# Twenty-four gate columns computed as rows of tokens beside the value columns, an earlier distance bias, and another order at both ends of a two-block transformer kernel

## The chip, the cores and the metric

The kernel runs on one core of a Trainium2 chip. The metric is the time of one launch on the device in microseconds (us). The engines are named as in the profile: PE (matrix engine; PEld is its weight load), DVE (vector), ACT (scalar), POOL (GpSimd), SP (issues most transfers). DVEq, ACTq, SPq are the queues on which an engine issues transfers.

## What is computed

Two transformer blocks over T = 512 tokens of width D = 1024, all in float32. The first block projects the normed rows and mixes two attentions, the second has a short convolution, a sparse attention with a distance bias and a feed-forward network. Of the first block, what matters here is:

```python
h = rms_norm(x, norm_g)
dq, dk, dv, dz, nq, nkv, nz, ng = jnp.split(h @ w_in, IN_SPLITS, axis=-1)   # dv: 512 columns, ng: 24
o_diff = diff_attention(rms_norm(dq), rms_norm(dk), dv, lam, slopes)
o_cmp, p_cmp = compressed_attention(nq, kc, vc)     # softmax over 31 compressed keys
...
g = jax.nn.sigmoid(ng)                              # three gates for each of 8 heads
o_nsa = g[0] * o_cmp + g[1] * o_slc + g[2] * o_win
x = x + concatenate([o_diff * silu(dz), o_nsa * silu(nz)]) @ w_out
```

Of the second block it is `bias = rel_bias[rel_bucket(distance)]`, a table of 32 x 8 looked up at 640 distances, made in the kernel as a product with a one-hot matrix, and at the very end `rms_norm_2(x, g_final)`, written out by rows.

## The kernel before

**Products.** Every projection is split so that float32 is kept: an operand is its rounded part (hi) plus the rest (lo), and a product of a 128-row k-tile is three matmuls, hi with hi, lo with hi, hi with lo (L1847). Weights come in units of up to 2048 columns per partition (1 MB). For each unit SP loads `raw` (two slots, used in turn), ACT rounds it to `w_hi` (L1084), POOL subtracts to get `w_lo` in pieces of 512 columns (L1024), and PE multiplies. For units that run beside an attention DVE makes the low pieces (L1703) instead. Two layouts exist. In a feature unit the weights are stationary and the 512 tokens move, so a tile is (up to 128 features) x 512. In a token unit (`token=True`) 128 tokens are stationary and the columns of the weights move; its four tiles are (128 tokens) x (columns).

**Order of work.** A plan is built in Python and each engine walks it. `order` (L208) lists the units, `project` emits the matmuls of a unit in steps of `size` k-tiles, and each step calls `tick`. What follows a unit is put in with `later(n, ...)`, n steps on. Each engine executes its entries strictly in plan order, waiting on semaphores.

**Units around the change.** After the NSA queries (`nq_u`) come the gate unit `ng_u` (the 24 gate columns with 96 neighbours, 120 columns as features, which makes tiles of 120 x 512), the NSA keys `nk_u` (kind `kd`), the two units of differential values `dv_u` (token units of 4 k-tiles x 512 columns), then the NSA values `nv_u` beside the differential attention.

- Gates: ACT takes the tanh of the tile (L1114), PE turns it by four transposes (L1874), DVE scales the turned 128 x 96 block into `ngt` (L1465).
- Norms of queries and keys (`NORM`): ACT squares (L1116, L1117, L1119), PE sums over the 64 rows of a head (L1888), ACT takes the root (L1146, L1147; the square root needs a table load where another function came between), DVE inverts (L1452, 128 x 512), POOL multiplies (L1034). For `kd`, DVE multiplies too (L1457, two of 64 x 512).
- Compressed scores: `scores(b)` for b = 0, 1. Part 0 is 16 matmuls on PE (32 records, L2056), part 1 masks and subtracts the maximum on DVE (L1599 to L1605), part 2 is the exponential on ACT (L1301), part 3 on DVE sums, inverts, multiplies with the gate and scales (L1609, L1610, L1612, L1614, L1615).
- The differential attention's first scores (L1906) follow the last value unit.

**Start.** PE runs 18 idle products as warm-up (L2064, 36 records), with the transpose of the first norm's gains after the 13th (L2067). DVE copies these gains (L1364), squares token row tile 1 (L1678) and scales the four row tiles (L1641); PE transposes them (L1798). Small arrays come by SP in a row of transfers (L958). The distance bias is made in the first projection: two products of `relb` with `onehot` (L2122, four records), copied by ACT (L1311).

**Tail of the NSA attention.** `split_high` and `split_low("mix", m)` make the hi and lo parts of the mixed rows for the output projection; the low part is DVE's L1737, which runs in plan order among the copies of turned probabilities (L1543) for which PE's products (L1978) wait.

**End.** The last product fills the final 256 columns in a tile of tokens. DVE and ACT scale the last row tile by halves of 512 columns (L1658, L1153), and SP issues two transfers, L1008 and then L1010.

## Time and profile before

| what | us |
|---|---|
| median of 3 runs | 1067.86 (1067.71 to 1067.88) |
| the profiled execution, its own time | 1068.18 |
| its span | 1066.4 |
| PE busy (5457 matmul records) | 1055.5 (99%) |
| PEld busy | 835.8 (78%) |
| DVE busy | 499.6 (47%) |
| ACT busy | 458.9 (43%) |
| POOL busy | 400.5 (38%) |
| chain that ended last: PE / DVE / ACT | 91% / 5% / 2% |

The profiled execution took 1.8 us more than its span, and 0.3 us more than the median of the runs. The busy time of a matmul record is modelled and overlaps its neighbour's; what a matmul costs in a stream is the distance from its start to the next one's start. The granted clock of PE was 1.00 in all 40 slices.

### The profile page before, as it was taken

What the parts mean: (1) busy time and instruction counts of PE and PEld (TensorE: products, weight loads), DVE (VectorE), ACT (ScalarE), POOL (GpSimd) and SP (SyncE); (2) the same over time, 40 slices, a digit from 0 to 9 for tenths busy, and PEclk for the clock granted to TensorE, in tenths of its full rate; (3) what the DMA queues carried; (4) which work ended last, traced back from release to release, by engine and by line L of the source; (5) the groups of instructions that cost most, each with busy time, mean ns of one, the idle gap of its engine ahead of it and who ended that gap; (6) DMA issues with size and microseconds to landing.
All of it is one profiled execution on the core that took longest, in us unless ns stands there. A gap on an engine that the chain in (4) does not pass through costs nothing.

```text
span 1066.4 us, 14261 instructions
## 1 busy us (share of the span) xinstructions
PE 1055.5 (99%) x5457; PEld 835.8 (78%) x5457; DVE 499.6 (47%) x1047; ACT 458.9 (43%) x789; POOL 400.5 (38%) x300
## 2 busy tenths in 40 slices
PE   9999999999999999999999999999999999999997
PEld 7777776867678876888777888888888888888886
DVE  5754798675671515998588235240000000032444
ACT  6455657676663524323366423342222122233533
POOL 3554630001023352545100154533534444465772
PEclk9999999999999999999999999999999999999999
DMA  9532221111123232232221223223232332322221
...
DMA packets 83667, 96.09 MB, mean 90 GB/s; under 512 B 8089, under 2 KB 68722, under 8 KB 83610
## 3 DMA queue, kind: packets, MB, share of 16 engines
...
## 4 chain that ended last, share of the span: by engine, by line
PE 91%; DVE 5%; ACT 2%; issue 1%; POOL 0%; DVEq 0%; ACTq 0%; POOLq 0%
PE bank L1847 54%; PE bank L2160 22%; PE bank L1906 4%; PE bank L1937 3%; PE bank L1978 3%; DVE L L1452 1%; PE bank L1954 1%; PE bank L1798 1%; PE bank L2135 1%; PE bank L2011 1%; DVE L L1502 1%; PE bank L2064 1%; PE bank L1888 0%; DVE w_lo L1703 0%; DVE pool L1457 0%
## 5 line engine op out<-in xcount | busy, mean ns | idle before, releaser
L1024 POOL TENSOR_TENSOR w_lo<-raw,w_hi 128x512 fp32r<-128x512 f32 (+1 forms) x190 | 268.4, 1442 | 440.6 <-ACT w_hi L1084 428.2
L1847 PE MATMUL bank<-h_hi,w_hi 128*128 128x512 f32 (+1 forms) x584 | 234.6, 402 | 0.5 <-POOL w_lo L1024 0.4
L1847 PE MATMUL bank<-h_hi,w_lo 128*128 128x512 f32 (+1 forms) x584 | 228.1, 391 | 0.0
L1847 PE MATMUL bank<-h_lo,w_hi 128*128 128x512 f32 (+1 forms) x584 | 227.2, 390 | 0.0
L1084 ACT ACTIVATE w_hi<-raw 128x512 fp32r<-128x512 f32 (+3 forms) x94 | 112.0, 1221 | 119.2 <-PE bank L1847 116.8
L1062 POOL TENSOR_TENSOR w_lo<-raw,w_hi 128x512 fp32r<-128x512 f32 x88 | 110.7, 1290 | 133.5 <-ACT w_hi L1329 67.1
L2160 PE MATMUL bank<-h_hi,w_hi 128*128 128x512 f32 x352 | 137.1, 389 | 0.0
L2160 PE MATMUL bank<-h_hi,w_lo 128*128 128x512 f32 x352 | 137.0, 389 | 0.0
L2160 PE MATMUL bank<-h_lo,w_hi 128*128 128x512 f32 x352 | 136.8, 389 | 0.0
L1847 PEld LDWEIGHTS bank<-h_hi,w_hi 128*128 128x128 f32 (+1 forms) x584 | 109.2, 187 | 34.0 <-issue 9.6
L1847 PE MATMUL bank<-w_hi,h_hi 128*128 128x512 f32 x333 | 129.8, 390 | 0.0
L1847 PE MATMUL bank<-w_hi,h_lo 128*128 128x512 f32 x333 | 129.6, 389 | 0.0
L1847 PE MATMUL bank<-w_lo,h_hi 128*128 128x512 f32 x333 | 129.6, 389 | 0.0
L1847 PEld LDWEIGHTS bank<-h_hi,w_lo 128*128 128x128 f32 (+1 forms) x584 | 109.2, 187 | 24.1
L1847 PEld LDWEIGHTS bank<-h_lo,w_hi 128*128 128x128 f32 (+1 forms) x584 | 109.4, 187 | 21.7 <-DVE h_lo L1745 0.4
L1783 DVE TENSOR_TENSOR pool<-bank,L 128x512 f32 (+1 forms) x22 | 15.2, 692 | 215.7 <-PE bank L2160 215.7
L2160 PEld LDWEIGHTS bank<-h_hi,w_hi 128*128 128x128 f32 x352 | 66.1, 188 | 14.0 <-ACT h_hi L1285 0.2
L2160 PEld LDWEIGHTS bank<-h_hi,w_lo 128*128 128x128 f32 x352 | 66.1, 188 | 13.7
L2160 PEld LDWEIGHTS bank<-h_lo,w_hi 128*128 128x128 f32 x352 | 66.1, 188 | 13.6
L1232 ACT ACTIVATE L<-L,st 128x128 f32<-128x128 f32 (+3 forms) x128 | 70.3, 555 | 13.5 <-DVE st L1502 13.5
L1847 PEld LDWEIGHTS bank<-w_hi,h_hi 128*128 128x128 f32 x333 | 62.5, 188 | 13.8 <-issue 1.0
L1847 PEld LDWEIGHTS bank<-w_lo,h_hi 128*128 128x128 f32 x333 | 62.5, 188 | 13.0
...
## 6 DMA issues: line engine op xcount, KB each, us to landing
...
```

The costliest lines, as they stand in the source:

```text
L1024: nc.gpsimd.tensor_tensor(w_lo[:, u.n % 2, cols], raw[:, u.n % 2, cols], w_hi[:, u.n % 2, cols].bitcast(F32), ALU.subtract).then_inc(lo_do ...
L1062: nc.gpsimd.tensor_tensor(w_lo[:, n % 2, cols], raw[:, n % 2, cols], w_hi[:, n % 2, cols].bitcast(F32), ALU.subtract).then_inc(lo_done, 1)
L1084: act_fn(w_hi[:, u.n % 2, cols], raw[:, u.n % 2, cols], ACT.Copy).then_inc(hi_done, 1)
L1232: ins = act_fn(x, x, ACT.Exp, scale=-1.0, bias=stat(ST_MN, job, c, p), accum_out=stat(ST_SM, job, c, p))
L1452: v.reciprocal(r, r).then_inc(recip_done, 1)
L1502: ins = v.tensor_tensor_reduce(out=x, in0=src, in1=bias, scale=factor, scalar=3e38, op0=ALU.add, op1=ALU.min, accum_out=stat(ST_MN, job, c ...
L1783: v.tensor_tensor(x, bank[2 + j][:, :], L[:, j, :], ALU.mult).then_inc(act_done, 1)
L1847: ins = mm(bank[t.bank][0:t.m, :], stationary, moving, start=first and n == 0, stop=last and n == len(products) - 1, skip_group_check=u.token)
L1906: ins = mm(bank[S_BANKS[c]][:, columns(job, p)], q, k, start=True, stop=True)
L1937: ins = nc.tensor.transpose(dst[:, o:o + P], L[:, (job.r + c) % LRING, o:o + P], ident)
L1978: ins = mm(O[DH * half:DH * half + DH, P * i:P * i + P], x, turned(job.t + half)[:, o:o + P], start=dsa and j == 0, stop=j == i and (dsa o ...
L2160: ins = mm(bank[2 * j + m][:, :], w[:, k, P * m:P * m + P], x[:, k, :], start=n == 0, stop=n == len(products) - 1)
```

## The change

1. The gate unit is gone. The 512 value columns come in three token units in place of two: 8 k-tiles x 256 columns, then twice 4 k-tiles x 280 columns (256 of the values and the 24 of the gates, loaded by a second transfer). ACT evacuates 256 columns of each tile and takes the tanh of the 24 straight into `ngt`; DVE scales `ngt` once (`gates`).
2. Part 3 of the compressed scores moves: b = 0 behind the differential attention, b = 1 ten steps later, inside the NSA attention. `scores(0)` and `scores(1)` come two steps later each.
3. The bias products move behind 14 idle products (18 before), the transpose after the 10th; `relb` and `onehot` are loaded by ACT's queue instead of SP's; DVE makes the two copies between token row tiles 0 and 1.
4. In the tail of the NSA attention the four `split_low` go from steps 4, 5, 6, 7 (each behind the step) to behind 5, behind 6, before 7 and behind 7, in the order m = 0, 1, 2, 3.
5. At the end the halves are 384 columns for ACT and 640 for DVE, and ACT issues the transfer of its own part.

```diff
-    ng_u = Unit("nsa_gate", [(rows_of(w1in, 0, ND, C_NG - 96, 120), 0, 120)], ND, 120, [Tile(0, 120, "ng", 0)])
-    dv_u = token_units("diff_v", w1in, C_DV, "dv", 0)
+    dv_u = [Unit("diff_v", [(rows_of(w1in, 0, ND, C_DV, 256), 0, 256)], ND, 256,
+                 [Tile(0, P, "dv", (0, i)) for i in range(NT)], token=True)]
+    gate_tiles = [Tile(0, P, "dv_ng", (1, i)) for i in range(NT)]
+    dv_u += [Unit("diff_v_nsa_gate", [(rows_of(w1in, k, 4, C_DV + 256, 256), 0, 256), (rows_of(w1in, k, 4, C_NG, 24), 256, 24)],
+                  4, 280, gate_tiles, k0=k, first=k == 0, last=k == 4, token=True) for k in (0, 4)]
...
-    order = (dq_u[:1] + [kv_u] + dk_u[:1] + dq_u[1:] + dk_u[1:] + nq_u + [ng_u, nk_u] + dv_u + [nv_u] + nz_u + z_u
+    order = (dq_u[:1] + [kv_u] + dk_u[:1] + dq_u[1:] + dk_u[1:] + nq_u + [nk_u] + dv_u + [nv_u] + nz_u + z_u
...
-    NORM, AUX_COPY = ("dq", "dk", "nq", "kd"), ("vd", "ng", "viw")
+    NORM, AUX_COPY = ("dq", "dk", "nq", "kd"), ("vd", "viw")
...
-            return
-        if group[0].kind == "ng":
-            later(2, lambda: [aux(t) for t in group])
-            later(4, lambda: [finish(t) for t in group])
...
+    left[0], left[4] = [("rows_done", 1)], [("rows_done", 2)]
...
-        bias_tiles = []
         col_waits, left[COL_BANK] = left[COL_BANK], [("col_done", 2)]
-        for j in range(2):
-            t = Tile(0, DSA_HEADS, "rows", j)
-            t.bank, t.waits = 6 + j, left[6 + j]
-            t.done = upto("tile_done")
-            left[t.bank] = [("rows_done", j + 1)]
-            bias_tiles.append(t)
-        emit("small_arrays", tiles=bias_tiles, waits=col_waits)
+        emit("small_arrays", waits=col_waits)
...
         emit("cmp", b=b, part=0, waits=waits)
-        for part in range(1, 4):
+        for part in range(1, 3):
             later(part, lambda part=part: emit("cmp", b=b, part=part, waits=None))
     later(2, cmp_values)
-    project(nq_u + [ng_u], RING4, 4)
-    later(1, lambda: scores(0))
-    later(5, lambda: scores(1))
-    project([nk_u] + dv_u, RING4, 4)
+    project(nq_u, RING4, 4)
+    later(3, lambda: scores(0))
+    later(7, lambda: scores(1))
+    project([nk_u], RING4, 4)
+    project(dv_u, RING4, 8)
...
     attend("diff", steps_left["diff"])
+    emit("gates")
+    emit("cmp", b=0, part=3, waits=None)
+    later(10, lambda: emit("cmp", b=1, part=3, waits=None))
...
             split_high("mix", at - 1)
+        if at == 7:
+            split_low("mix", 2)
         attend("nsa")
-        if 4 <= at < 8:
-            split_low("mix", at - 4)
+        if 5 <= at < 8:
+            split_low("mix", (0, 1, 3)[at - 5])
...
-        LAST_BANK = 4
+        LAST_BANK, LAST_COLS = 4, 384
...
+        table_in, rows_mm = sem("table_in"), sem("rows_mm")
...
-            sp.dma_start(out[0, T - P:T, 512:D], zs[:, NT - 1, 512:D]).then_inc(out_done, 16)
-            sp.wait_ge(y_act, NT)
-            sp.dma_start(out[0, T - P:T, 0:512], zs[:, NT - 1, 0:512]).then_inc(out_done, 16)
+            sp.dma_start(out[0, T - P:T, LAST_COLS:D], zs[:, NT - 1, LAST_COLS:D]).then_inc(out_done, 16)
...
-                    act_fn(dv[:, idx[1], :], src, ACT.Copy).then_inc(sc_evac, 1)
+                    act_fn(dv[:, idx[1], 0:256], src[:, 0:256], ACT.Copy).then_inc(sc_evac, 1)
+                if kind == "dv_ng":
+                    act_fn(dv[:, idx[1], 256:T], src[:, 0:256], ACT.Copy)
+                    act_fn(ngt[:, idx[1], :], src[:, 256:280], ACT.Tanh, scale=0.5).then_inc(sc_evac, 1)
...
             def scaled(i):
-                x = zs[:, i, 0:D if i < NT - 2 else 512]
+                x = zs[:, i, 0:D if i < NT - 2 else LAST_COLS]
                 sc.wait_ge(recip_last, i + 1)
                 act_fn(x, x, ACT.Copy, scale=st[:, ST_RR + i:ST_RR + i + 1]).then_inc(y_act, 1)
+                if i == NT - 1:
+                    sc.wait_ge(y_act, NT)
+                    sc.dma_start(out[0, T - P:T, 0:LAST_COLS], x).then_inc(out_done, 16)
...
             sc.dma_start(vec_rows[R_NORM:R_NORM + ND, :], a["norm_g"][0].rearrange("(r c) -> r c", c=P)).then_inc(first_in, 16)
+            sc.dma_start(relb[:, :], a["rel_bias_2"]).then_inc(table_in, 16)
+            sc.dma_start(onehot, a["onehot"]).then_inc(table_in, 16)
...
-                    for j, t in enumerate(e["tiles"]):
-                        w = T if j == 0 else BIASW - T
-                        sc.wait_ge(tile_done, t.done)
-
-                        act_fn(bias_row[:, T * j:T * j + w], bank[t.bank][0:DSA_HEADS, 0:w], ACT.Copy, scale=-1.0)\
-                            .then_inc(rows_done, 1)
...
-                elif t.kind == "ng":
-                    v.tensor_scalar(ngt[:, :, :], blocks[:, :, 96:120], 0.25, 0.25, ALU.mult, ALU.add).then_inc(aux_copied, 1)
...
                     ve.wait_ge(recip_last, i + 1)
-                    v.tensor_scalar(zs[:, i, 512:D], zs[:, i, 512:D], r, None, ALU.mult).then_inc(y_done, 1)
+                    x = zs[:, i, LAST_COLS:D]
+                    v.tensor_scalar(x, x, r, None, ALU.mult).then_inc(y_done, 1)
...
                     normed_row(nth, i)
+                    if i == 0:
+                        for j, w in enumerate((T, BIASW - T)):
+                            ve.wait_ge(rows_mm, j + 1)
+                            v.tensor_scalar(bias_row[:, T * j:T * j + w], bank[4 * j][0:DSA_HEADS, 0:w], -1.0, None, ALU.mult)\
+                                .then_inc(rows_done, 1)
...
                                            ALU.mult, ALU.mult).then_inc(kc_done, 1)
+                if kind == "gates":
+                    ve.wait_ge(sc_evac, gate_tiles[-1].sc)
+                    chain(v.tensor_scalar(ngt[:, :, :], ngt[:, :, :], 0.25, 0.25, ALU.mult, ALU.add))
...
-                        pe.wait_ge(sc_evac, dv_u[1].tiles[-1].sc)
+                        pe.wait_ge(sc_evac, gate_tiles[-1].sc)
...
             pe.wait_ge(zero_done, 1)
-            for n in range(18):
+            for n in range(14):
                 mm(bank[4][:, 0:P], idle_rows, idle_rows, start=True, stop=True)
-                if n == 12:
+                if n == 13:
+                    pe.wait_ge(table_in, 32)
+                    for j, w in enumerate((T, BIASW - T)):
+                        mm(bank[4 * j][0:DSA_HEADS, 0:w], relb[:, :], onehot[:, T * j:T * j + w], start=True, stop=True)\
+                            .then_inc(rows_mm, 1)
+                if n == 9:
...
-                    for j, t in enumerate(e["tiles"]):
-                        w = (T, BIASW - T)[j]
-                        wait_free(pe, t.waits)
-                        mm(bank[t.bank][0:DSA_HEADS, 0:w], relb[:, :], onehot[:, T * j:T * j + w], start=True, stop=True)\
-                            .then_inc(tile_done, 1)
```

What the planner does with it stands in the rows of the program's order. First **POOL from the NSA queries to the end of the values**. `pool<-pool,L` is the norm multiplication of two query tiles, `pool<-zs,L` that of the two key tiles, eight or four `w_lo` pieces are one or two units. Before:

```order
L1024 TENSOR_TENSOR w_lo<-raw,w_hi 128x512 [waits hi_done]
L1024 TENSOR_TENSOR w_lo<-raw,w_hi 128x448 [waits hi_done]
L1034 TENSOR_TENSOR pool<-pool,L 128x512 [waits ve_evac,recip_done] x2
L1024 TENSOR_TENSOR w_lo<-raw,w_hi 128x512 [waits hi_done] x8
L1034 TENSOR_TENSOR pool<-pool,L 128x512 [waits ve_evac,recip_done] x2
L1024 TENSOR_TENSOR w_lo<-raw,w_hi 128x512 [waits hi_done] x4
L1034 TENSOR_TENSOR pool<-zs,L 128x512 [waits ve_evac,recip_done] x2
L1024 TENSOR_TENSOR w_lo<-raw,w_hi 128x512 [waits hi_done] x4
```

And with the change:

```order
L1020 TENSOR_TENSOR w_lo<-raw,w_hi 128x512 [waits hi_done] x4
L1030 TENSOR_TENSOR pool<-pool,L 128x512 [waits ve_evac,recip_done] x2
L1020 TENSOR_TENSOR w_lo<-raw,w_hi 128x512 [waits hi_done] x4
L1030 TENSOR_TENSOR pool<-pool,L 128x512 [waits ve_evac,recip_done] x2
L1020 TENSOR_TENSOR w_lo<-raw,w_hi 128x512 [waits hi_done] x2
L1020 TENSOR_TENSOR w_lo<-raw,w_hi 128x96 [waits hi_done]
L1030 TENSOR_TENSOR pool<-zs,L 128x512 [waits ve_evac,recip_done] x2
L1020 TENSOR_TENSOR w_lo<-raw,w_hi 128x512 [waits hi_done] x2
L1020 TENSOR_TENSOR w_lo<-raw,w_hi 128x96 [waits hi_done]
L1020 TENSOR_TENSOR w_lo<-raw,w_hi 128x512 [waits hi_done] x4
```

Before, all weights of the values were split ahead of the key norm's two multiplications. Now those of the third value unit (the second row pair of 512 and 96) stand behind them.

**ACT, with the change, from the first value unit to the third** (L1120 evacuates 256 value columns, L1303 is the exponential of the compressed scores, L1143 and L1144 are the key norm's roots, L1080 the high part of the third value unit):

```order
L1120 ACTIVATE pool<-bank 128x256 [waits tile_done]
L1303 ACT_TABLE_LOAD
L1303 ACTIVATE pool<-pool 128x16x31 [waits cmp_lg_done]
L1120 ACTIVATE pool<-bank 128x256 [waits tile_done]
L1143 ACT_TABLE_LOAD
L1143 ACTIVATE L<-bank,st 64x512 [waits aux_done]
L1144 ACTIVATE L<-bank,st 64x512
L1143 ACTIVATE L<-bank,st 64x512
L1144 ACTIVATE L<-bank,st 64x512
L1120 ACTIVATE pool<-bank 128x256 [waits tile_done] x2
L1080 ACTIVATE w_hi<-raw 128x1120 [waits tile_done,raw_in0]
```

The key roots now stand behind the second token tile of the first value unit; before, they stood behind no evacuation of a value tile.

**DVE inside the NSA attention, with the change** (L1527 scales probabilities, L1603 to L1609 are part 3 for b = 1, L1621 scales the differential output, L1496 takes PE's next scores):

```order
L1527 TENSOR_SCALAR L<-L,st 128x256 [waits dve_step]
L1527 TENSOR_SCALAR L<-L,st 128x256 x3
L1603 TENSOR_REDUCE st<-pool 128x16 [waits cmp_ex_done]
L1604 RECIPROCAL st<-st 128x16 [waits dve_step]
L1606 TENSOR_TENSOR st<-st,ngt 128x16 [waits dve_step]
L1608 TENSOR_TENSOR pool<-pool,const 128x16x31 [waits dve_step]
L1609 TENSOR_TENSOR pool<-pool,st 128x16x31 [waits dve_step]
L1621 TENSOR_TENSOR pool<-pool,st 128x512 [waits diff_recip]
L1703 TENSOR_TENSOR w_lo<-raw,w_hi 128x512 [waits hi_done]
L1496 ISA L,st<-bank,pool 128x512 [waits tr_done,s_done]
```

Before, the rows L1603 to L1609 (there L1609 to L1615) were not in this place; L1627, L1703 and L1502, their counterparts there, followed directly on the four L1533.

## Rows read from the trace of the kernel before

**Rows 1.** PE's waits (us, times, longest us); then the page's loads (busy, mean ns).

```profile
PE bank L1906 <- DVE st L1502: 1.6, 5, 0.5
...
PE bank L1798 <- DVE zs L1641: 0.9, 1, 0.9
PE bank L1978 <- DVE pool L1543: 0.5, 1, 0.5
PE bank L1847 <- POOL w_lo L1024: 0.4, 1, 0.4
...
L1847 PEld LDWEIGHTS bank<-h_hi,w_hi 128*128 128x128 f32 (+1 forms) x584 | 109.2, 187 | 34.0 <-issue 9.6
```

**Rows 2.** Chain in three windows: start us, us, what.

```profile
17.22 1.17 PE bank L2122 x4
...
118.69 1.91 PE bank L2056 x32
...
123.54 0.41 PE bank L1874 x4
...
427.52 95.42 PE bank L1847 x420
```

**Rows 3.** Busy time in 1058.08 to 1060.12 us: length, PE, PEld, DVE, ACT, POOL, clock, DMA.

```profile
1058.08:1060.12 2.04, 2.04 (x19) 2.03 (x17) 1.68 (x4) 1.81 (x4) 0.00 (x0) 1.00 0.63 257
```

**Rows 4.** PE's timeline: start us, us, what, [idle before <-releaser].

```profile
114.86 0.40 PE L1847 MATMUL bank<-h_hi,w_lo 128*120 128x512 f32 x1
115.70 0.47 PE L1847 MATMUL bank<-h_hi,w_hi 128*128 128x512 f32 x1 [0.44 <-POOL w_lo L1024]
...
154.27 1.14 PE L1906 MATMUL bank<-pool 64*128 64x128 f32 x8
...
231.90 1.14 PE L1906 MATMUL bank<-pool 64*128 64x128 f32 x8
```

**Rows 5.** POOL's timeline.

```profile
122.01 5.04 POOL L1024 TENSOR_TENSOR w_lo<-raw,w_hi 128x512 fp32r<-128x512 f32 x4 [2.72 <-ACT w_hi L1084]
...
132.72 5.87 POOL L1024 TENSOR_TENSOR w_lo<-raw,w_hi 128x512 fp32r<-128x512 f32 x4 [2.73 <-ACT w_hi L1084]
142.47 1.79 POOL L1034 TENSOR_TENSOR pool<-zs,L 128x512 f32<-128x512 f32 x1 [3.88 <-DVE L L1452]
```

**Rows 6.** ACT's timeline, a table load and a root.

```profile
115.91 1.28 ACT L1146 ACT_TABLE_LOAD   x1
117.21 0.68 ACT L1146 ACTIVATE L<-bank,st 64x512 f32<-64x512 f32 x1
```

**Rows 7.** DVE's timeline around 140 and 150 us.

```profile
139.04 3.34 DVE L1452 RECIPROCAL L<-L 128x512 f32<-128x512 f32 x1
142.42 2.38 DVE L1457 TENSOR_TENSOR pool<-zs,L 64x512 f32<-64x512 f32 x2
...
150.64 0.67 DVE L1609 TENSOR_REDUCE st<-pool 128x16 f32<-128x496 f32 x1
...
153.15 2.49 DVE L1703 TENSOR_TENSOR w_lo<-raw,w_hi 128x512 fp32r<-128x512 f32 x4
```

**Rows 8.** DVE's timeline in the NSA attention.

```profile
210.23 0.69 DVE L1397 SCALAR_TENSOR_TENSOR zs<-zs,bank 128x512 f32<-128x512 f32 x1 [2.18 <-ACT zs L1124]
...
230.28 0.69 DVE L1502 CUSTOM_DVE_ANT_0 L<-bank,pool 128x512 f32<-128x512 f32 x1 [0.45 <-PE bank L1937]
```

**Rows 9.** DVE's timeline at the start.

```profile
7.16 0.17 DVE L1364 COPY col<-bank 128x8 f32<-128x8 f32 x1 [6.28 <-PE bank L2067]
7.24 1.22 DVE L1678 CUSTOM_DVE_ANT_0 zs<-xres 128x1024 f32<-128x1024 f32 x1
...
11.76 1.01 DVE L1641 TENSOR_SCALAR zs<-xres,st 128x128 f32<-128x128 f32 x3
```

**Rows 10.** The end: ACT's last operation and the last transfer's issue.

```profile
1062.77 0.72 ACT L1153 ACTIVATE zs<-zs,st 128x512 f32<-128x512 f32 x1 [0.23 <-DVE st L1655]
...
1063.67 0.43 SPq L1010 DMA_DIRECT2D out<-zs  x1
```

10 lines of the change are left out of this document (3 added, 7 removed).

## The prediction

> **What bounds it now.** I read first the busy shares (PE 99% of the span), then PE's waits. Behind its warm-up PE stands still on nothing but four pairs of lines [rows 1]: at the start for `zs`, at one weight unit for POOL's `w_lo`, five times for DVE's scores in the attentions, once for the copies of turned probabilities. They make 3.4 us in all. So the time is the sum of what PE streams, and the change is worth what it takes from or adds to that stream, plus the waits that it opens or closes. What other engines save is worth nothing unless PE waits for them. PE's stream has a fixed pace: in a long stretch of 512-column matmuls 420 take 95.42 us [rows 2], so one costs 0.227 us.
>
> **The sum, part by part.**
>
> *The gate unit goes.* It has 8 k-tiles x 3 products = 24 matmuls of 512 tokens; 24 x 0.227 = 5.45 us. Its four transposes are 0.41 [rows 2]. Both lie in PE's stream: **-5.86**. With them go the tanh, DVE's scaling of a bank and 960 columns of `w_lo`, all off the path, at 0, with one exception: the norm multiplication and the next unit's `w_lo` came too late for PE at 115.70. The last gate matmul starts at 114.86, and 0.227 later the next should have [rows 4]: 0.6 us lost. POOL's work comes in another order now (four `w_lo` pieces of the keys, then the queries' two multiplications), so the piece no longer stands behind DVE's inverse: **-0.6**.
>
> *The value units.* Before: 2 units x 4 k-tiles x 4 token tiles x 3 = 96 matmuls of 512 columns, 21.8 us. After: 96 of 256 and 96 of 280. The only narrow matmuls of this kind are in the last unit: between the first start at 1058.08 and the last at 1060.12 lie 17 intervals (the row counts 19 records, a neighbour's among them), 0.120 us each [rows 3]. For 280 I take 0.130 (0.120 x 280/256). 96 x 0.120 + 96 x 0.130 = 24.0: **+2.2**.
>
> *Bias products.* Their four records take 1.17 us of the first projection [rows 2] and move to the time in which PE waits for `zs` (0.9 us, plus four idle products fewer): **-1.2**. The new hazard: they wait for two transfers issued on ACT's queue among the large loads of the rows.
>
> *The start.* DVE idles 6.28 us until PE has turned the gains, and squares row 1 right behind, for 1.22 us [rows 9]. The transpose comes three idle products sooner, so this chain can start about 1 us earlier. But DVE now copies the bias between rows 0 and 1 (two operations; 0.3 to 0.7 us each by the copy of 8 columns, 0.17 [rows 9], and the 512-column one of 0.69 [rows 8]) and may wait there for the bias products, with the scaling of rows 1 to 3 queued behind. Row 3 starts at 11.76 now [rows 9]. Bounds -1.0 (the whole head start) and +1.0 (the table loads as late as the last row tile); I take **-0.4**, since rows 1 to 3 also wait for their own loads.
>
> *A new wait at the third value unit.* Its `w_lo` stands behind the key norm's multiplications on POOL, and these behind ACT's roots, which now stand behind the evacuation of the first value unit's second token tile. From the end of that tile the chain is: evacuation and hand-overs 0.3; table load 1.28 and a pair of roots 2 x 0.69 [rows 6]; inverse 3.34, DVE's multiplications 2.38, second inverse 3.34 [rows 7]; POOL's multiplication 1.79 and one piece of `w_lo` 1.47 as beside a busy DVE, 5.87/4 [rows 5]. That is 15.3 us. PE meanwhile does token tiles 2 and 3 (2 x 24 x 0.120 = 5.8), the second unit (48 x 0.130 = 6.2) and compressed scores (1.91 [rows 2]): 13.9. So it arrives 1.4 us early, and the second piece, needed two k-tiles in, costs about 0.9 more: **+2.3**. Bounds: 0 if ACT gets the roots out earlier, 3.5 if each step slips by a few tenths. The high part of the NSA values, behind the second exponential on ACT, has the third unit's 6.2 us as cover.
>
> The Trainium skill, "SBUF — State Buffer", section "SBUF: two separate sides", says that the port pair of VectorE and GpSimd is an exclusive lock and the loser blocks for a whole instruction. Here POOL's multiplication ran 1.79 us while DVE's two took 2.38, started 0.05 apart [rows 5, 7]: against 5.04/4 = 1.26 for one of POOL's operations of this size undisturbed: slower by 0.5, not blocked. By the rule, `w_lo` would wait for one more whole DVE multiplication, 1.2 us, and this term would be 3.3 or so.
>
> *Part 3 of the compressed scores.* It is taken from DVE ahead of the first differential scores (2.50 us for b = 1, 150.64 to 153.15 [rows 7]), where DVE was close behind PE but never waited for. It is put into the NSA attention. For b = 0 (2.75 with the scaling of the gates) there is a cover: DVE idles 2.18 us before 210.23 [rows 8], and the half microsecond left over falls before PE's next need. For b = 1 DVE's chain runs to the products of 231.90 [rows 4] with only 0.45 idle [rows 8] and about 1.0 us between its last score and PE's need. 2.5 - 0.45 - 1.0 = **+1.1**. Bounds 0 and 2.5.
>
> *Tail of the attention.* PE waits 0.5 us once for DVE's copy L1543 [rows 1], which stands behind two low parts. Moved earlier, they leave it free: **-0.6** with the restart; bounds -0.7 and 0 (the moved ones may block an earlier copy).
>
> *The end.* ACT's last operation, 512 columns, ends at 1063.49; SP issues the last transfer at 1063.67 [rows 10]. With 384 columns it is about 0.1 shorter, and ACT issues at once: **-0.2**. DVE's 640 columns add under 0.1 and end before ACT.
>
> Sum: -5.86 - 0.6 + 2.2 - 1.2 - 0.4 + 2.3 + 1.1 - 0.6 - 0.2 = **-3.3 us**; in the profile 1068.2 becomes 1064.9. That execution was 0.3 above the median of the runs, so against the median: 1067.86 - 3.3 = **1064.6**.
>
> **Rivals.** A difference under 0.2%, 2.1 us, is about what a measurement of this kernel cannot tell from none.
>
> 1. *The waits eat the gain.* Third value unit 3.5, part 3 of b = 1 2.5, no head start: -3.3 + 1.2 + 1.4 + 0.4 = -0.3, **1067.5**, no change. For it: two serial chains were priced without slack. Against: all would have to go wrong together.
> 2. *No new waits.* If ACT and DVE run ahead in both places and the start gains 1.0: -3.3 - 2.3 - 1.1 - 0.6 = -7.3, **1060.6**. For it: PE's waits on DVE are few now [rows 1]. Against: the chain of 15.3 us consists of measured steps.
> 3. *Slower: narrow matmuls are paced by their weight loads.* A token unit of 256 columns needs as many weight loads as one of 512. In the last unit PEld is busy 2.03 of 2.04 us with 17 loads [rows 3], 0.12 a load, so that queue is full there. If PE could not start the next load before the last one's whole 0.187 us [rows 1] were over, 192 x 0.187 = 35.9 in place of 24.0: +11.9, the result +8.6, **1076.5**. It decides from a spacing of 0.153 us: (3.3 + 2.1)/192 = 0.028 above the mean of 0.125. Against it: the same row shows 19 matmuls in 2.04 us, which no pace of 0.187 allows. The Trainium skill, "TensorE: Matmul & The Clock Gate", section "Back-to-back issue gap", says that spacing is set by both operations, the load and the matmul; the row agrees with loads overlapping each other or the matmul here. It is a short stretch, though, and a stream of 192 is not seen.
>
> **Numbers.** The forecast's own case 0.50, with 1063.0 to 1065.7 as its range; no new waits 0.25; waits eat the gain 0.20; narrow matmuls 0.05. Faster: 0.50 + 0.25 = 0.75; within 0.2%: 0.20; slower: 0.05. The range takes in the forecast, most of rivals 1 and 2, and leaves out rival 3 and the ends of the others: 1061.4 to 1067.4.
>
> **What would show it.** Matmul starts 0.120 and 0.130 us apart in the value units, 24 matmuls and 4 transposes fewer. No PE wait on `w_lo` at the key unit, but one of 1 to 2.5 us at the third value unit, with the key norm's multiplications ending just before on POOL. PE's first scores about 3.6 us earlier than 154.27 [rows 4] (5.86 + 0.6 + 1.2 + 0.4 less 2.2 and 2.3). A wait of about 1 us on DVE near 230 behind part 3, and none on L1543 in the tail. The forecast is wrong if the narrow matmuls are over 0.14 apart, or if the bias transfers land late and PE starts its transposes after 9.4.

## The result: 0.24% slower, where 0.3% faster was predicted

| | before | with the change |
|---|---|---|
| median of 12 runs each, us | 1067.88 (1067.71 to 1068.31) | 1070.57 (1069.17 to 1071.36) |
| profiled execution, its own time, us | 1068.18 | 1070.57 |
| its span, us | 1066.4 | 1068.7 |

The ratio is 1.0024 [1.0016, 1.0032]: slower by 2.7 us, where -3.3 was forecast. So 6 us have to be found. The executions also spread over 2.2 us instead of 0.6, and the mean granted clock of PE is 0.994 to 0.997 in them, where the profiled execution of before had 1.00.

**The waits.** With the change, PE's waits and the load that stood in [rows 1] (columns as there):

```profile
PE bank L1909 <- DVE st L1496: 2.8, 6, 1.1
PE bank L1850 <- POOL w_lo L1020: 2.5, 2, 1.9
...
PE bank L2071 <- DMA PT<-in_onehot: 0.8, 1, 0.8
PE bank L1801 <- DVE zs L1635: 0.8, 1, 0.8
PE bank L1909 <- ACT ngt L1123: 0.6, 1, 0.6
PE bank L1850 <- ACT h_hi L1287: 0.2, 1, 0.2
...
L1850 PEld LDWEIGHTS bank<-h_hi,w_hi 128*128 128x128 f32 (+1 forms) x576 | 107.7, 187 | 32.9 <-issue 10.3
```

The wait for DVE's copy in the tail is gone; the one for `w_lo` went from 0.4 to 2.5 and now lies at the third value unit; four are new: `onehot`, `ngt`, a short one of 0.2 for `h_hi` ahead of the first projection, and a sixth of 1.1 on L1909. Together they are 7.7 us against 3.4, so 4.3 more, in a stream that is shorter by 3.8 (5.86 us of gate matmuls and transposes less, 2.1 more in the values). That makes +0.5; the other 1.8 us of the 2.3 between the spans lie where no wait is listed.

**The start.** The chain that ended last, 0 to 16 us (start us, us, what):

```profile
2.16 6.25 DMA PT<-in_onehot
...
8.46 1.03 PE bank L2071 x2
...
9.52 0.88 DVE L L1680 x2
...
10.50 0.76 DVE zs L1635
...
11.31 3.30 PE bank L1801 x16
```

and DVE's timeline (start, length, what, [idle before]), which answers to [rows 9]:

```profile
5.88 0.17 DVE L1360 COPY col<-bank 128x8 f32<-128x8 f32 x1 [5.00 <-PE bank L2075]
...
9.52 0.88 DVE L1680 TENSOR_SCALAR L<-bank 8x512 f32<-8x512 f32 x2 [1.43 <-PE bank L2071]
...
10.50 0.75 DVE L1635 TENSOR_SCALAR zs<-xres,st 128x1024 f32<-128x1024 f32 x1
```

The gains are copied 1.28 us sooner (5.88 against 7.16). But the bias products stood for `onehot`, which had taken 6.25 us to land; DVE's copies stood for the products, and the scaling of row 1 (10.50) behind the copies. DVE wins its head start at the gains and loses all of it, and more, at 9.52.

How large the head start is depends on the warm-up, and this pair shows it at its largest. PE's timeline of the kernel before, and that of a later version with the same start (the tail undone, below):

```profile
1.00 5.91 PE L2064 MATMUL bank<-vc 128*128 128x128 f32 x26 [1.00 <-POOL vc L1036]
```

```profile
1.00 4.68 PE L2073 MATMUL bank<-vc 128*128 128x128 f32 x26 [1.00 <-POOL vc L1039]
```

The same 26 records took 5.91 us before, and 4.68 to 5.01 in the four profiled executions of later versions with the old start (start undone, all four repaired, end undone, tail undone). Those copied the gains at 5.88 to 6.21 instead of 7.16, so against them the 5.88 above is 0.0 to 0.3 sooner. They also passed the place of the first projection where before is at 18.32 at 17.87 to 18.06. So the profiled execution of before is 0.3 to 0.5 us behind them at the start, and what is read against it makes the change look better by as much.

**The clock.** Busy time in six stretches (columns as in [rows 3]; the number behind POOL's is the granted clock):

```profile
10.00:12.00 2.00, 1.20 (x8) 0.96 (x7) 1.93 (x6) 1.87 (x5) 0.00 (x0) 0.66 1.10 364
12.00:14.00 2.00, 2.00 (x11) 2.00 (x11) 1.19 (x5) 0.03 (x1) 0.62 (x1) 0.50 0.64 182
...
146.00:148.00 2.00, 1.00 (x4) 0.77 (x5) 1.93 (x3) 0.00 (x0) 2.00 (x3) 0.80 0.00 0
148.00:150.00 2.00, 2.00 (x10) 2.00 (x10) 0.80 (x3) 1.66 (x3) 0.39 (x1) 0.50 0.25 36
150.00:152.00 2.00, 2.00 (x15) 2.00 (x15) 1.45 (x4) 1.52 (x5) 0.00 (x0) 0.85 1.01 332
...
1060.29:1062.33 2.04, 2.04 (x19) 2.03 (x17) 1.68 (x4) 1.81 (x4) 0.00 (x0) 1.00 0.63 257
```

Twice PE falls to the lower of its two levels (0.50, 1.2 GHz) at a pair of standstills: the two of 0.8 us at the start, and those of the third value unit. In finer windows the fall comes at about 10.7 and 147.2, each time just after the second standstill has begun. Before, both stretches were at 1.00. No wait is recorded for it: PE is "busy" 2.00 of 2.00 us and does half the work. The last row answers to [rows 3] and is the same as there, record for record.

**The value units.** PE's timeline:

```profile
123.75 0.28 PE L1850 MATMUL bank<-w_hi,h_hi 128*128 128x256 f32 x1
...
126.15 0.28 PE L1850 MATMUL bank<-w_lo,h_hi 128*128 128x256 f32 x1
...
139.00 0.29 PE L1850 MATMUL bank<-w_hi,h_hi 128*128 128x280 f32 x1
...
142.08 0.29 PE L1850 MATMUL bank<-w_hi,h_hi 128*128 128x280 f32 x1
...
144.26 0.29 PE L1850 MATMUL bank<-w_lo,h_hi 128*128 128x280 f32 x1
146.42 0.40 PE L1850 MATMUL bank<-w_hi,h_hi 128*128 128x280 f32 x1 [1.87 <-POOL w_lo L1020]
...
147.66 0.60 PE L1850 MATMUL bank<-w_hi,h_hi 128*128 128x280 f32 x1 [0.58 <-POOL w_lo L1020]
148.06 0.43 PE L1850 MATMUL bank<-w_hi,h_lo 128*128 128x280 f32 x1
148.29 0.43 PE L1850 MATMUL bank<-w_lo,h_hi 128*128 128x280 f32 x1
...
155.59 1.14 PE L1909 MATMUL bank<-pool 64*128 64x128 f32 x8 [0.56 <-ACT ngt L1123]
...
234.43 1.14 PE L1909 MATMUL bank<-pool 64*128 64x128 f32 x8 [1.12 <-DVE st L1496]
```

From 123.75 to 126.15 are 20 intervals, 0.120 each; from 139.00 to 142.08 are 24, 0.128 each. At 148 one takes 0.23. The last two rows answer to [rows 4]. The first value matmul starts at 123.40, where it started at 129.27 before.

What PE waited for at 146.42 stands in POOL's timeline, and what POOL waited for in DVE's (beside [rows 5, 7]):

```profile
137.10 1.79 POOL L1030 TENSOR_TENSOR pool<-zs,L 128x512 f32<-128x512 f32 x1 [7.75 <-DVE L L1448]
142.90 1.78 POOL L1030 TENSOR_TENSOR pool<-zs,L 128x512 f32<-128x512 f32 x1 [4.01 <-DVE L L1448]
144.64 3.74 POOL L1020 TENSOR_TENSOR w_lo<-raw,w_hi 128x512 fp32r<-128x512 f32 x3
```

```profile
133.66 3.35 DVE L1448 RECIPROCAL L<-L 128x512 f32<-128x512 f32 x1 [5.82 <-ACT L L1144]
...
139.47 3.35 DVE L1448 RECIPROCAL L<-L 128x512 f32<-128x512 f32 x1
```

The first inverse starts behind ACT's roots (L1144), which a table load at 130.96 precedes; then the second inverse, POOL's multiplication and `w_lo` follow: the chain of the prediction, link by link.

**The end.** ACT's last operation and its transfer, beside [rows 10]:

```profile
1065.05 0.62 ACT L1150 ACTIVATE zs<-zs,st 128x384 f32<-128x384 f32 x1 [0.23 <-DVE st L1649]
1065.69 0.37 ACTq L1153 DMA_DIRECT2D out<-zs  x1
```

**Where the difference stands.** The same events of PE in both traces, as start with the change less start before: +0.86 in the first projection (19.18, 18.32), +0.83 at 99.80, +1.32 at the first scores (155.59, 154.27), +1.33 at 210.39, +2.53 at the scores of 234.43 (231.90), +2.07 in the output projection (313.51, 311.44), +2.21 at the last matmul (1062.33, 1060.12), +2.3 in the span. The start, the values, part 3 and the tail each have their step in this list. Against the four other executions of the old start the step of the start is 1.1 to 1.3 rather than 0.86.

### The profile page after: what moved, and what is told of

It reads as the page before. It is cut to its first block, busy times and chain, and to the rows that moved or that the text cites. A ratio compares the mean times of both kernels' runs of the same rounds, so it can differ in the third digit from the quotient of the medians.

```text
span 1068.7 us, 14387 instructions
## 1 busy us (share of the span) xinstructions
PE 1053.5 (99%) x5517; PEld 839.2 (79%) x5517; DVE 497.5 (47%) x1049; ACT 455.2 (43%) x792; POOL 399.3 (37%) x300
## 4 chain that ended last, share of the span: by engine, by line
PE 93%; DVE 3%; ACT 2%; issue 1%; DMA 1%; POOL 0%; ACTq 0%; DVEq 0%
PE bank L1850 56%; PE bank L2163 22%; PE bank L1909 4%; PE bank L1940 3%; PE bank L1981 3%; PE bank L1957 1%; PE bank L2138 1%; PE bank L1801 1%; DVE L L1496 1%; PE bank L2014 1%; PE bank L1891 1%; DVE L L1448 1%; DMA PT<-in_onehot 1%; PE bank L1970 0%; PE bank L1933 0%
## 5 line engine op out<-in xcount | busy, mean ns | idle before, releaser
L1850 PE MATMUL bank<-h_hi,w_hi 128*128 128x512 f32 (+1 forms) x576 | 231.3, 402 | 0.3 <-ACT h_hi L1287 0.2
L1850 PE MATMUL bank<-h_hi,w_lo 128*128 128x512 f32 (+1 forms) x576 | 225.0, 391 | 0.0
L1850 PE MATMUL bank<-h_lo,w_hi 128*128 128x512 f32 (+1 forms) x576 | 224.0, 390 | 0.0
L1080 ACT ACTIVATE w_hi<-raw 128x512 fp32r<-128x512 f32 (+3 forms) x94 | 111.4, 1214 | 114.0 <-PE bank L1850 113.2
L1850 PE MATMUL bank<-w_hi,h_hi 128*128 128x512 f32 (+2 forms) x365 | 136.7, 374 | 2.5 <-POOL w_lo L1020 2.5
L1850 PE MATMUL bank<-w_hi,h_lo 128*128 128x512 f32 (+2 forms) x365 | 136.1, 373 | 0.0
L1850 PE MATMUL bank<-w_lo,h_hi 128*128 128x512 f32 (+2 forms) x365 | 136.0, 373 | 0.0
L1850 PEld LDWEIGHTS bank<-w_hi,h_hi 128*128 128x128 f32 x365 | 69.3, 190 | 15.6 <-POOL w_lo L1020 2.9
L1850 PEld LDWEIGHTS bank<-w_hi,h_lo 128*128 128x128 f32 x365 | 69.2, 190 | 11.8
L1850 PEld LDWEIGHTS bank<-w_lo,h_hi 128*128 128x128 f32 x365 | 69.2, 190 | 11.8
```

The lines of the kernel that those rows point to most:

```text
L1080: act_fn(w_hi[:, u.n % 2, cols], raw[:, u.n % 2, cols], ACT.Copy).then_inc(hi_done, 1)
L1850: ins = mm(bank[t.bank][0:t.m, 0:u.width if u.token else T], stationary, moving, start=first and n == 0, stop=last and n == len(products) ...
```

## The experiments

Diffs are against the changed kernel, unless said otherwise. The kernel before ran beside each, with medians of 1067.8 to 1068.0. A difference "against the change" is against 1070.57.

**The start undone.** `relb` and `onehot` back on SP's queue, the bias products in the first projection, the copies by ACT, 18 idle products.

```diff
-            for n in range(14):
+            for n in range(18):
...
-                if n == 9:
+                if n == 12:
...
-            sc.dma_start(relb[:, :], a["rel_bias_2"]).then_inc(table_in, 16)
-            sc.dma_start(onehot, a["onehot"]).then_inc(table_in, 16)
...
+                small(relb[:, :], a["rel_bias_2"])
+                small(onehot[:, :], a["onehot"])
```

> The changed kernel with the start of the kernel before: 18 idle products, the bias products inside the first projection, the two table loads in SP's row of small loads, the copies on ACT. In the changed kernel PE begins the first projection at 15.46 us (13.30 before) and stands 0.86 us behind after the bias products are accounted for. If the start is worth only what is seen there, this run gains 0.8 to 1.0 us on the changed kernel (about 1069.7), its granted clock stays at full speed up to 20 us, and its times scatter less than the 2.2 us of the changed kernel's twelve runs, because no chain hangs on the landing of a small transfer. Rival: the start is not the cause of the loss, and this run stays within 0.3 us of the changed kernel's 1070.6.

Measured: 1069.45 (1067.90 to 1070.66, 11 runs), ratio 1.0015 [1.0006, 1.0024]. The start costs 1.1 us, it does not gain; the intervals of the two kernels overlap, and the same start on the kernel before, further down, gives the same price. The profiled execution was the fastest, 1067.90, and the other ten took 1069.26 or more. A window and PE's timeline at the third value unit show why that is worth a look:

```profile
146.00:148.00 2.00, 1.56 (x12) 1.57 (x13) 0.91 (x1) 1.05 (x3) 1.17 (x2) 1.00 0.00 0
```

```profile
145.20 0.40 PE L1857 MATMUL bank<-w_hi,h_hi 128*128 128x280 f32 x1 [1.87 <-POOL w_lo L1028]
...
146.44 0.40 PE L1857 MATMUL bank<-w_hi,h_hi 128*128 128x280 f32 x1 [0.58 <-POOL w_lo L1028]
```

The same two waits, and the clock stayed at 1.00. So the fall is no certain consequence of the waits. The mean clock of the other ten was 0.996 to 0.998, of this one 0.998; their stretches were not profiled.

**The roots earlier.** Steps of four k-tiles in the value units let the key norm's roots come ahead of ACT's evacuations.

```diff
-    later(7, lambda: scores(1))
+    later(11, lambda: scores(1))
...
-    project(dv_u, RING4, 8)
+    project(dv_u, RING4, 4)
```

> The changed kernel with the steps of the value units cut to 4 k-tiles, as before, and the second compressed scores four steps later so that they keep their place: the key norm's sums and roots come one token tile earlier. Theory: PE's two waits at the third value unit (1.87 and 0.58 us by the profile) and the 3.4 us at half clock behind them are one event, caused by the chain of roots, inverses and multiplications ahead of the unit's low parts; all of it goes, 2.8 us of waits and 1.3 us of slow matmuls, so this run gains about 4 us (about 1066.5) and the clock stays full from 100 to 160 us. Rival: the narrow matmuls lower the clock by themselves; then the waits go (2.8 us) but the granted clock still falls somewhere in the value units.

Measured: 1067.29 (1065.14 to 1068.23, 11 runs), ratio 0.9992 [0.9983, 1.0001], 3.3 less than the change. The waits for `w_lo` fell from 2.5 to 0.6 us, and the clock was 1.00 throughout 140 to 158 us. 1.9 of wait and 1.3 of clock are the 3.2.

**Banks shifted, before the keys.** Meant to move the tile that the first scores wait for.

```diff
+    turn[RING4] += 3
     project([nk_u], RING4, 4)
```

> The changed kernel with the ring of four PSUM banks turned by one before the key unit, so that the last token tile of the values no longer lies in bank 3, for which the first differential scores wait. Theory: the 0.56 us wait of PE's scores for the tanh of the last 24 gate columns (0.7 us with the restart) is a matter of the bank; it goes, and the run gains 0.6 to 0.8 us (about 1069.9). Rival: the scores need the last evacuation for another reason; then PE's line of the scores still waits for that line and nothing is gained.

Measured: 1079.87 (1079.14 to 1081.46, 4 runs), ratio 1.0109. PE's waits:

```profile
PE bank L1851 <- DVE pool L1390: 5.1, 1, 5.1
...
PE bank L1851 <- ACT pool L1137: 1.6, 2, 0.8
```

A miss as a test: it gave the keys themselves banks that were not free yet, and says nothing on the first scores. It shows only that a shift of the PSUM banks has its price (6.7 us in these two rows). One thing in its trace bears on the clock: PE stood 1.87 and 0.57 us at the third value unit, as with the change, and the clock was 1.00 from 150 to 160 us.

**18 idle products again, bias products at their end.**

```diff
-            for n in range(14):
+            for n in range(18):
...
-                if n == 13:
+                if n == 17:
```

> The changed kernel with four more idle products ahead of the bias products (18 as before, the transpose after the 10th as in the change). PE would otherwise stand still there from 7.6 to 8.46 us. Theory of the clock: the two standstills of 0.84 and 0.80 us one behind the other let the clock fall to half at 10.8 us until 14.1 us, and this costs more than the waiting itself; with the first one filled the clock stays full, the 28 transposes take as long as before, and the run gains 1.0 to 1.6 us. Rival: what costs is the late landing of the table alone; then the row of the granted clock may change but the first projection begins at 15.3 to 15.5 us all the same, since the row tiles are scaled late.

Measured: 1069.42 (1068.92 to 1070.92, 11 runs), ratio 1.0017 [1.0008, 1.0026]. In the profiled execution the waits are the same as with the change (`onehot` 0.8, `zs` 0.8), but the clock is not:

```profile
10.00:12.00 2.00, 1.20 (x10) 0.97 (x10) 1.93 (x6) 1.89 (x5) 0.00 (x0) 1.00 1.10 365
```

The first projection starts at 14.36 in place of 15.46, though the bias products began 0.2 later (8.68 against 8.46). So at least 1.1 us of the start is the clock alone. That the idle products kept it up is not shown: the table landed so late that PE stood 0.76 us all the same, and with 14 idle products two profiled executions (bank order, middle repaired) also had a clock of 1.00 here behind the same two standstills. The median is 1.15 lower, no more than the scatter of the two kernels can make. This execution then lost at the third value unit, at 0.50 from 146 until after 152, and took 1070.88. The runs fall into two groups: 1068.92 to 1069.42 at a mean clock of 0.997 (six), 1070.62 to 1070.92 at 0.995 to 0.996 (five).

**The values' banks in another order.** The last token tile no longer lies in the bank that the first scores take first.

```diff
-    project(dv_u, RING4, 8)
+    project(dv_u[:1], RING4, 8)
+    project(dv_u[1:], (0, 1, 3, 2), 8)
```

> The changed kernel with the banks of the last value tiles taken in the order 0, 1, 3, 2, so that the last token tile lies in bank 2 and the one before it in bank 3. The earlier trial turned the ring ahead of the key unit and moved the keys' own banks with it, so it could not answer this. Theory: the first differential scores wait for the tile in bank 3; it is now evacuated a token tile (1.5 us) earlier, their 0.56 us wait on the tanh of the last 24 columns is gone, and the run gains 0.5 to 0.8 us (about 1069.9). Rival: the wait stays, because the scores need the last tile whatever its bank.

Measured: 1069.89 (1068.39 to 1071.27, 11 runs), ratio 1.0018 [1.0009, 1.0027]: 0.7 less than the change, and the wait of 0.6 for `ngt` is gone, with the other waits as they were. The trace shows it; a difference of 0.7 between medians is by itself within the scatter of both kernels. In this execution the clock was at 1.00 until 146 us, though PE had stood 0.90 and 0.80 at the start.

**The standstill filled.** Fourteen records of idle products ahead of the third value unit, released by the key norm's last root. The wait stays, only PE is not still in it.

```diff
                 wait_free(pe, t.waits)
+                if u is dv_u[2] and j == 0:
+                    pe.wait_ge(aux_root, nk_u.tiles[1].root)
+                    for _ in range(7):
+                        mm(bank[4][:, 0:P], ident, ident, start=True, stop=True)
```

> The changed kernel with seven idle products (128 x 128) put ahead of the third value unit, where PE stood still for 1.87 us; they take about 1.9 us, and the low parts arrive as late as before. Theory: standing still is what lets the clock fall there, so the clock stays full, the unit's matmuls are 0.13 us apart instead of 0.23, and the run gains 1.0 to 1.6 us though nothing that it waits for comes sooner; its times scatter less. Rival: the slow matmuls come from POOL's and DVE's reading of the same weights or from narrow matmuls as such; then they stay 0.23 apart and nothing is gained.

Measured: 1068.96 (1067.20 to 1070.28, 11 runs), ratio 1.0009 [1.0000, 1.0018], 1.6 less than the change with more work on PE. PE's timeline:

```profile
145.25 1.72 PE L1833 MATMUL bank<-const 128*128 128x128 f32 x14
147.28 0.40 PE L1854 MATMUL bank<-w_hi,h_hi 128*128 128x280 f32 x1 [0.31 <-POOL w_lo L1020]
...
148.52 0.40 PE L1854 MATMUL bank<-w_hi,h_hi 128*128 128x280 f32 x1 [0.58 <-POOL w_lo L1020]
148.75 0.30 PE L1854 MATMUL bank<-w_hi,h_lo 128*128 128x280 f32 x1
```

The second wait is unchanged, and the clock is 1.00 in every window from 144 to 154 us. One trace proves little here, since two without the idle products (start undone, banks shifted) kept 1.00 as well; it is the median of 11 runs that speaks for the filling.

**Part 3 of b = 1 later still.**

```diff
-    later(10, lambda: emit("cmp", b=1, part=3, waits=None))
+    later(18, lambda: emit("cmp", b=1, part=3, waits=None))
```

> The changed kernel with part 3 of the compressed scores for b = 1 eighteen steps on instead of ten, where DVE idles 2.8 us before 265 us and where its result is still in time. Theory: the 1.12 us that PE waits for DVE at 234.4 us is this part alone; it goes and the run gains 1.1 to 1.3 us. Rival: DVE is late there for another reason (the scaling of the differential output), or the wait comes back at 265 us; then 0.3 us or less is gained.

Measured: 1068.88 (1067.79 to 1070.33, 11 runs), ratio 1.0010 [1.0001, 1.0019]. The waits on DVE are 1.7 us in five in place of 2.8 in six, so the one of 1.1 is gone. The median fell by 1.7; of this the trace explains 1.1, and the rest is no more than the scatter of either kernel.

**All four repaired:** start undone, roots earlier, bank order, part 3 later.

```diff
-    later(7, lambda: scores(1))
+    later(11, lambda: scores(1))
...
-    project(dv_u, RING4, 8)
+    project(dv_u[:1], RING4, 4)
+    project(dv_u[1:], (0, 1, 3, 2), 4)
...
-    later(10, lambda: emit("cmp", b=1, part=3, waits=None))
+    later(18, lambda: emit("cmp", b=1, part=3, waits=None))
```

> The start of the kernel before, and in the rest of the changed kernel the three repairs together: roots a token tile earlier, the banks in the order 0, 1, 3, 2, part 3 of b = 1 eighteen steps on. If the four causes are separate and add up, this takes 1.1 + 3.3 + 0.7 + 1.2 = 6.3 us from the changed kernel's 1070.6, about 1064.3, 3.6 us under the kernel before, and the times scatter by less than 0.7 us as those of the kernel before do. If they overlap (a wait that only moves on to the next), it ends at 1066 to 1067.

Measured: 1064.15 (1063.91 to 1064.21, 5 runs), ratio 0.9965 [0.9951, 0.9978]. PE's waits:

```profile
PE bank L1917 <- DVE st L1509: 1.7, 5, 0.5
...
PE bank L1858 <- POOL w_lo L1029: 0.6, 1, 0.6
PE bank L2129 <- DMA pool<-in_distance: 0.5, 1, 0.5
```

6.4 less than the change; the four alone gave 1.1 + 3.3 + 0.7 + 1.7 = 6.8. The spread is 0.3 us and the mean clock 0.999. The middle of the change is worth having once its waits are gone.

**The new start alone, on the kernel before.** Against the kernel before:

```diff
+            sc.dma_start(relb[:, :], a["rel_bias_2"]).then_inc(table_in, 16)
+            sc.dma_start(onehot, a["onehot"]).then_inc(table_in, 16)
...
-            for n in range(18):
+            for n in range(14):
...
+                if n == 13:
+                    pe.wait_ge(table_in, 32)
```

> The kernel before with nothing of the change but its start: 14 idle products, the bias products behind them, the table loads on ACT's queue, DVE's copies between rows 0 and 1. Taking this start out of the changed kernel gained 1.1 us. If the start costs that by itself, this run is 0.8 to 1.5 us slower than the kernel before (about 1069.0), PE waits for the one-hot table until after 8.1 us, and its times scatter by 1.5 us or more, the slower ones with the lower mean clock. Rival: the loss was an interplay with the value units; then this run is within 0.3 us of the kernel before.

Measured: 1069.18 (1068.42 to 1070.22, 11 runs), ratio 1.0012 [1.0003, 1.0021]: 1.2 slower by itself. PE waits 1.4 for `onehot`, and its clock is 0.50 from 10 to 12 us.

**Start repaired on the new layout:** tables issued first on ACT's queue, 18 idle products, the copies behind row 3; the middle repaired as above.

```diff
-            sc.dma_start(ident, a["const"][:, K_IDENT:K_IDENT + P]).then_inc(first_in, 16)
-            sc.dma_start(vec_rows[R_NORM:R_NORM + ND, :], a["norm_g"][0].rearrange("(r c) -> r c", c=P)).then_inc(first_in, 16)
             sc.dma_start(relb[:, :], a["rel_bias_2"]).then_inc(table_in, 16)
             sc.dma_start(onehot, a["onehot"]).then_inc(table_in, 16)
+            sc.dma_start(ident, a["const"][:, K_IDENT:K_IDENT + P]).then_inc(first_in, 16)
+            sc.dma_start(vec_rows[R_NORM:R_NORM + ND, :], a["norm_g"][0].rearrange("(r c) -> r c", c=P)).then_inc(first_in, 16)
```

> The middle repaired as in the run of all repairs (1064.15), and the changed kernel's start kept, but with the tables issued first on ACT's queue, 18 idle products ahead of the bias products and DVE's two copies behind the last row tile. Theory: the 6.3 us in flight of the one-hot table are queueing behind the 2 MB of rows; issued ahead of them it lands before 6 us, PE never stands still for it, the clock stays full, and the bias products' 1.17 us leave the first projection: 1062.8 to 1063.6. Rival: the projection then waits for the small arrays instead, which land no sooner; then the run stays at 1064.0 to 1064.3.

Measured: 1069.13 (1066.93 to 1069.93, 11 runs), ratio 1.0004 [0.9995, 1.0013]. The expectation fell. The runs lie in two groups, five at 1066.93 to 1067.27 and six at 1069.13 to 1069.93, and the profiled one is the fastest. The chain at the start:

```profile
2.15 6.17 DMA PT<-in_norm_g
...
8.62 0.17 DVE col L1361
```

Now the gains are the fourth transfer of that queue, and they are the late ones: 2.15 + 6.17 = 8.32, where they had been in time for a copy at 5.88 as the second. It is the place in the queue that is late, not the table: 6.2 us for 4 KB issued at 2.15, while the 80 KB of `onehot`, now second, took 4.8 us. PE stood 2.8 us for the gains.

**The end undone,** on the kernel with all four repaired: halves of 512 columns, the last transfer by SP.

```diff
-        LAST_BANK, LAST_COLS = 4, 384
+        LAST_BANK, LAST_COLS = 4, 512
...
+            sp.wait_ge(y_act, NT)
+            sp.dma_start(out[0, T - P:T, 0:LAST_COLS], zs[:, NT - 1, 0:LAST_COLS]).then_inc(out_done, 16)
...
-                if i == NT - 1:
-                    sc.wait_ge(y_act, NT)
-                    sc.dma_start(out[0, T - P:T, 0:LAST_COLS], x).then_inc(out_done, 16)
```

> The kernel of all repairs (1064.15) with the end of the kernel before: halves of 512 columns, both transfers issued by SP. The prediction put the new end at 0.2 us gained; the profile of the changed kernel shows the last issue 0.19 us earlier against the last matmul, but a longer flight. If the end is worth 0.2 us this run is at 1064.3 to 1064.4; if the flight from ACT's queue gives it back, at 1064.0 to 1064.2.

Measured: 1064.02 (1063.72 to 1064.28, 5 runs) against 1064.15. The new end gains nothing that these runs could show.

**The tail undone,** on the same kernel.

```diff
-        if at == 7:
-            split_low("mix", 2)
...
-        if 5 <= at < 8:
-            split_low("mix", (0, 1, 3)[at - 5])
+        if 4 <= at < 8:
+            split_low("mix", at - 4)
```

> The kernel of all repairs (1064.15) with the low parts of the mixed rows in the order of the kernel before. Theory: the wait of PE's products for DVE's copy of turned probabilities comes back, 0.5 us with its restart, and the run is at 1064.5 to 1064.8. Rival: the wait comes back but the next unit waited for its low parts anyway; then 1064.1 to 1064.3.

Measured: 1064.67 (1064.60 to 1064.81, 6 runs) against 1064.15: +0.5, and the wait of 0.5 for DVE's copy of turned probabilities (L1548 there) is back.

**The middle repaired, the new start kept:** the diff of all four above, but not the start. This isolates the start from the clock's fall at the value units.

> The changed kernel with the three repairs of the middle (roots a token tile earlier, bank order, part 3 of b = 1 later) and its new start untouched. Against the run with the old start (1064.15) it prices the new start alone: if that costs 1.1 us by itself this is 1065.3, with a scatter of 1.5 us or more that comes from the start alone, the runs at the lower mean clock being the slow ones. Rival: the scatter and 1 us of loss came from the value units; then it lies at 1064.0 to 1064.5 with little scatter.

Measured: 1065.34 (1063.41 to 1065.90, 11 runs), ratio 0.9974 [0.9965, 0.9983]: 1.2 above the version with the old start. The profiled execution took 1063.47, with its clock at 1.00 everywhere, though PE stood 0.7 us for `onehot` and 0.8 for `zs`:

```profile
10.00:12.00 2.00, 1.20 (x12) 1.08 (x11) 1.89 (x6) 1.87 (x5) 0.00 (x0) 1.00 1.09 365
```

So in its best executions (1063.47, and one of 1063.41) the new start is 0.7 better than the old (1064.15), and in the median it is 1.2 worse. The 1.9 us between them are not all the clock: this execution also had the earliest bias products of all with the new start (8.07, against up to 8.68). The stretches of the other executions were not profiled.

**Copies behind row 3,** and 18 idle products, on that kernel.

```diff
-                    if i == 0:
+                    if i == 3:
...
-            for n in range(14):
+            for n in range(18):
...
-                if n == 13:
+                if n == 17:
```

> The previous kernel (new start, middle repaired) with DVE's two copies of the bias behind the last row tile and 18 idle products ahead of the bias products; the table loads as in the change. If DVE's copies, queued and waiting ahead of rows 1 to 3, are what delays the projection, row 1 is scaled at 8.3 us instead of 10.5, the projection begins before 13.5 us, the bias products are hidden and the run is at 1062.8 to 1063.6. If the landing of the table on PE is the cause, PE still begins the transposes after 9.5 us and the run is at 1064.5 or above.

Measured: 1064.77 (1064.51 to 1064.99, 7 runs), ratio 0.9971. PE's timeline:

```profile
9.40 1.53 PE L1802 MATMUL bank<-const,zs 128*128 128x128 f32 x12
12.83 1.96 PE L1802 MATMUL bank<-const,zs 128*128 128x128 f32 x16 [1.90 <-DVE L L1681]
```

Row 1 was scaled two microseconds sooner, but the transposes need a bank that still holds the bias products, and now wait 1.9 for the copies. Neither expectation holds as it was reasoned, though the time is the rival's: the copies have to come early for the bank and late for DVE. The spread is 0.5 us, with the clock at 1.00, even behind the standstill of 1.90.

**Tables by ACT's queue, everything else of the start old,** on the kernel with all four repaired; a semaphore of their own, and the bias products wait for it in the first projection.

```diff
+            sc.dma_start(relb[:, :], a["rel_bias_2"]).then_inc(table_in, 16)
+            sc.dma_start(onehot, a["onehot"]).then_inc(table_in, 16)
...
+                    pe.wait_ge(table_in, 32)
                     for j, t in enumerate(e["tiles"]):
```

> The run of all repairs (old start, 1064.15) with the two tables on ACT's queue behind the gains, with a semaphore of their own, and the bias products ahead of PE's wait for the small arrays instead of behind it. PE waited 0.5 us there for the last small array; the products fill that, and SP's row is two transfers of 0.43 us shorter. Expected 1063.5 to 1063.8. Rival: the first weights of the projection, issued on SP behind the small ones, do not move and the 1.54 us wait of ACT for them (19.8 us) governs; then 1064.0 to 1064.2.

Measured: 1063.82 (1063.60 to 1064.37, 5 runs), ratio 0.9963 [0.9950, 0.9977]. Two transfers fewer in SP's row, and the wait of 0.5 for `distance` is gone. But the first projection is only 0.1 us ahead of the version with all four repaired at the same place (17.88 against 17.96), and 0.3 between medians is within the spread of these runs, so it is not shown to be faster. Together with the version with the end undone it is the fastest kernel here, 4.0 us below the kernel before.

## Why the prediction was wrong

The mechanisms were mostly the predicted ones; two terms had the wrong size, and two things were not in the sum at all.

| term | predicted | measured | from |
|---|---|---|---|
| gate unit, wait at 115.70 | -6.5 | -6.7, no wait left | first value matmul, 123.40 for 129.27, with the offset of 0.83 ahead of it |
| value units' pace | +2.2 | +2.1 | 0.120 and 0.128 us a matmul |
| bias products and start | -1.6 | +0.9 against this execution of before, +1.2 against four others of the old start and in medians | offset at 19.18; three experiments |
| third value unit | +2.3 | +2.8 wait, +1.3 clock, +0.2 restarts | PE's timeline |
| first scores wait for `ngt` | not seen | +0.7 | PE's timeline; bank order |
| part 3, b = 1 | +1.1 | +1.2 | offset 1.33 to 2.53; part 3 later |
| tail | -0.6 | -0.5 | offset 2.53 to 2.07; tail undone |
| end | -0.2 | 0 to +0.1 | end undone |

Budget of the middle, between 99.80 and 155.59, where the offset grows by 0.49: -6.7 + 2.1 + 2.8 + 1.3 + 0.2 + 0.7 = +0.4.

**Bias products and start: the step that failed most,** 2.5 to 2.8 us. The prediction named the hazard ("they wait for two transfers issued on ACT's queue among the large loads of the rows", "may wait there ... with the scaling of rows 1 to 3 queued behind"), set a bound of +1.0, and then took -0.4 with -1.2 for the products. The table landed at 8.41 and the chain behind it moved row 1's scaling from 9.43 to 10.50. PE's transposes began at 9.63, so the prediction's own sign, "after 9.4", stood in the trace.

Three things stand in place of the -1.6. First, the head start was read off one execution with a slow warm-up, where it is 1.28; against the four others of the old start it is 0.0 to 0.3, and either way it ended with row 0. Second, the copies behind the late table ate most of what moving the products saved, or all of it. At one place of the first projection (19.18 in the changed kernel's trace) those four stood at 17.87 to 18.06, and the new start with its clock at 1.00 at 17.45 (middle repaired), 17.73 (bank order) and 18.06 (18 idle products): a term of -0.5 to +0.1. Third, the clock: where it fell, the same place was passed at 18.67 to 19.18 (the change, roots earlier, the new start on the kernel before) and at 19.91 to 20.15 where PE had stood 1.6 us or more for the table. That is 2.7 us between executions of one start. That the new start costs time was shown three times (on the change, on the kernel before, on the repaired middle), at 1.1 to 1.2 us each; the one on the kernel before is the firmest, since the kernel beside it scatters by 0.6 us only.

**Third value unit: mechanism and place right, size off by 1.8.** The waits were 2.16 - 0.13 = 2.03 and, with the slower restart, 0.75; predicted were 1.4 and 0.9. What failed is that the sum had no price for the clock: the 12 intervals from 147.66 to 150.62 took 2.96 us where 12 of 0.129 are 1.55, of which 1.3 are the clock and 0.1 is the restart. With the standstill filled, `w_lo` as late as before and the clock at 1.00, the median was 1.6 lower, which points to PE standing still, and not to the wait as such. The prediction's "3.3 or so" for a whole DVE multiplication more should read 3.5 (2.3 and 1.2); POOL's multiplication took 1.78 us beside DVE's, so that one did not come about.

**The first scores: missed.** The gates now come out of the last token tile by ACT, behind 256 value columns, and that tile lies in a bank that the first scores write. The prediction looked at DVE ahead of these scores and not at who still reads the banks; the wait and its restart are 0.7 us. In its list of signs the first scores were to come 3.6 us earlier than 154.27; they came 1.3 later. The other bank order took the wait away.

**Right:** no wait at the key unit any more, the pace of narrow matmuls (rival 3 falls over a stream of 192: 0.12 to 0.13, far from 0.153), POOL's multiplications at 1.79 and 1.78 us beside DVE's (slowed, not blocked), the wait of about 1 us behind part 3, and the tail. Rival 1, "the waits eat the gain", described the outcome best, but its worst case, 1067.5, also had no clock in it, and it kept the -1.2 of the bias products. The measured 1070.57 lies above that and above the whole range, and far below rival 3's 1076.5.

**The end:** ACT issued its transfer at 1065.69, 3.36 us behind the last matmul, where SP's was 3.55 behind it: the 0.2 is there. But from the end of the issue to the end of the span were 2.6 us, against 2.3 before, and the gain is gone. The view of transfers agrees: ACT's 192 KB took 2.6 us from issue to landing, SP's last 256 KB 2.2 before. Why the smaller transfer takes longer was not tried.
